# A sixth expert's weights outside the ring of block one

## The reference, cut to what matters

```python
def first_block(x, mem, ...):
    h = rms(x, mix_norm_g)                    # latent attention beside Hyena convolutions
    x = x + mixed @ w_out
    x = x + cross_attention(rms(x), rms(mem)) @ w_mo
    x = x + hier_moe(rms(x, ffn_norm_g), ...) # 32 experts, 2 per token
    return rms(x, final_norm_g)

def expert(t, e):                             # for the tokens routed to e
    a, b = t @ w_gate[e], t @ w_up[e]         # 1024 -> 256 twice
    return (silu(a) * b * combine[t, e]) @ w_down[e]   # 256 -> 1024

def second_block(x, c, ...):                  # RG-LRU beside block attention
    mod = silu(c) @ w_ada + b_ada             # 1024 -> 6 * 1024, scales and shifts
    x = layernorm(alpha * x + g1 * mixer(modulate(x, sh1, sc1)))
    return layernorm(alpha * x + g2 * moe(modulate(x, sh2, sc2)))
```

## Time and profile before

| what | value |
| --- | --- |
| median of 3 runs | 940.55 us (939.97 to 941.27) |
| profiled execution | 940.86 us, span 939.0 us |
| TensorE busy | 873.3 us, 93% of the span |
| VectorE, ScalarE, GpSimd busy | 505.8, 349.3, 22.3 us |
| HBM read | 286.70 MB, 306 GB/s over the span |
| SyncE's transfers | 25632 packets, 281.40 MB, 73.3% of the 16 engines' span |
| mean granted clock of TensorE | 0.994 |

### The profile page before, as it was taken

One profiled execution on the slowest core, in us unless ns is written; L12 is line 12 of the kernel. 1 busy time (PEld: TensorE's weight loads), 2 busy tenths in 40 slices (PEclk: granted clock), 3 DMA queues, 4 the chain that ended last, 5 costly groups with the idle time before them and its releaser, 6 DMA issues.

```text
span 939.0 us, 15033 instructions
## 1 busy us (share of the span) xinstructions
PE 873.3 (93%) x5670; PEld 562.7 (60%) x5670; DVE 505.8 (54%) x1110; ACT 349.3 (37%) x688; POOL 22.3 (2%) x41
## 2 busy tenths in 40 slices
PE   8999999999999998987887899999899999999995
PEld 7778558888867633443333379876665545545452
DVE  5876578466345657333322485788754633333335
ACT  5684444456345222221121366743621111111113
POOL 1010110000000000000000000000000000000000
PEclk9999999999999999999999999999999999999998
DMA  9655881545407999999999978530729999999991
GB/s 359 252 207 199 343 329 66 195 176 214 179 1 308 415 414 423 424 423 427 425 426 424 421 263 364 224 136 1 312 76 394 424 423 427 427 424 425 425 424 67
DMA packets 29184, 288.43 MB, mean 307 GB/s; under 512 B 3112, under 2 KB 5576, under 8 KB 7888
## 3 DMA queue, kind: packets, MB, share of 16 engines
q1 hardware_dynamic: 25632, 281.40, 73.3%
q0 software_dynamic: 1136, 3.74, 1.2%
q10 hardware_dynamic: 2368, 2.64, 0.8%
HBM read 286.70 MB, written 1.06 MB: 306 GB/s over the span
## 4 chain that ended last, share of the span: by engine, by line
PE 58%; DMA 19%; DVE 14%; ACT 4%; issue 3%; SPq 1%; DVEq 0%; ACTq 0%
DMA ring<-in_experts 15%; PE bank L1107 12%; PE bank L1127 7%; PE bank L703 7%; PE bank L705 6%; PE bank L704 6%; PE bank L1155 5%; DVE ring_r L525 3%; PE bank L1112 2%; DMA arena<-in_mem 2%; PE bank L1066 2%; PE bank L1119 2%; DMA ring<-in_ada 1%; DMA ring<-in_lat 1%; PE bank L794 1%
## 5 line engine op out<-in xcount | busy, mean ns | idle before, releaser
L525 DVE TENSOR_TENSOR ring_r<-ring,ring_r 128x1024 fp32r<-128x1024 f32 (+1 forms) x84 | 99.2, 1211 | 66.7 <-ACT ring_r L518 66.5
L1107 PE MATMUL bank<-ring,arena 128*64 128x256 f32 x1056 | 121.2, 382 | 1.6 <-DMA ring<-in_experts 1.4
L518 ACT ACTIVATE ring_r<-ring 128x1024 fp32r<-128x1024 f32 (+1 forms) x84 | 85.0, 1046 | 68.3 <-PE bank L705 67.6
L703 PE MATMUL bank<-HT_r,ring_r 128*128 128x256 f32 x352 | 101.8, 289 | 4.6 <-DVE ring_r L525 3.8
L705 PE MATMUL bank<-HT_r,ring_r 128*128 128x256 f32 x352 | 99.6, 283 | 0.0
L1107 PEld LDWEIGHTS bank<-ring,arena 128*64 128x64 f32 x1056 | 74.2, 137 | 39.3 <-issue 6.2
L1127 PE MATMUL bank<-ring,arena 128*64 128x512 f32 (+1 forms) x512 | 96.7, 604 | 0.5 <-DVE arena L2492 0.3
L1723 ACT ACTIVATE arena<-bank 128x256 f32<-128x256 f32 (+1 forms) x65 | 31.8, 490 | 147.5 <-PE bank L1107 83.4
L1112 PE MATMUL bank<-ring,arena 128*32 128x512 f32 x496 | 59.6, 598 | 25.1 <-DMA ring<-in_experts 25.1
L704 PE MATMUL bank<-XN_r,ring_r 128*128 128x256 f32 x288 | 81.5, 283 | 0.0
L2465 DVE SCALAR_TENSOR_TENSOR arena<-bank,arena,HT 128x512 f32<-128x512 f32 x33 | 24.8, 750 | 101.5 <-PE bank L1127 101.5
(11 more groups left out here) (483 smaller groups left out, 1425.8 us busy)
## 6 DMA issues: line engine op xcount, KB each, us to landing
ring<-in_experts SPq DMA_DIRECT2D x64, 2048.0 KB, 16.6
ring<-in_experts SPq DMA_DIRECT2D x64, 1024.0 KB, 14.0
ring<-in_ada SPq DMA_DIRECT2D x12, 2048.0 KB, 8.8
ring<-in_win SPq DMA_DIRECT2D x5, 2048.0 KB, 12.2
ring<-in_hy SPq DMA_DIRECT2D x3, 2048.0 KB, 18.3
ring<-in_mk SPq DMA_DIRECT2D x2, 2048.0 KB, 13.4
ring<-in_mv SPq DMA_DIRECT2D x2, 2048.0 KB, 9.3
ring<-in_wo SPq DMA_DIRECT2D x2, 2048.0 KB, 8.1
```

The costliest lines, as they stand in the source:

```text
L518: nc.scalar.activation(R(h), w, ACT.Copy).then_inc(sem("w_high"), 1)
L525: nc.vector.tensor_tensor(R(w), w, R(h), ALU.subtract).then_inc(sem("w_low"), 1)
L703: mm(ps, R(ah), R(bh), start=first, stop=False)
L1107: last = mm(gu_bank[g * wide:(g + 1) * wide, 0:256], xw[:, k, :], w[k // 4][:, o:o + 256], start=k == 0, stop=k == KD - 1)
```

## The change

Six experts are held instead of five, so block one's ring has 30 places (`RUNG`) for its experts instead of 31.

- Expert 4's down half goes into ROW, issued first of all experts' parts (after `skip_z` and the transposed mix, both long past). Its gate and up half stays in XN and HT.
- Expert 5 lies outside too: down half in X, issued when the first sorting bank is full, gate and up half in the arena (two parts, when the last one is).
- ada8 and ada9 are summed in one bank as one set; the sum of both is evacuated to a piece of the arena. ada8's slot is free once its matmuls are done, ada9's once the bank is full. The first four experts are loaded in the order 2, 0, 1, 3.
- X is overwritten in the sorting, so the four banks of the sums are begun in the routing (two on each side of the counts) and steps 1 and 2 have a filler instead. These banks are 1 to 4, so the eight sorting banks are now four, each used twice (5, 6, 7, 0). ScalarE copies banks 0, 1, 2, 3, 4 and 6 of them, VectorE 5 and 7.
- final_norm_g's row, which lies in ROW, is loaded by GpSimd after expert 4's down matmuls and no longer after the mix.
- Expert e from 6 on lies in slot (e-2) modulo 4 of the experts' places. The extra rounds' slot is the one of expert 30 (before: 29), and SyncE's wait ahead of them asks for a count of 31 (before: 30).

The diff, cut to its core:

```diff
-RUNG = [NE - 1, NE]
+RUNG = [NE - 2, NE]
...
-        + [(f"gx{b}", 8, ((3, 4, 5, 6, 7, 0, 1, 2), (4, 5, 6, 7, 4, 5, 6, 7))[b - 1])] \
+        + [(f"gx{b}", 8, ((5, 6, 7, 0, 5, 6, 7, 0), (4, 5, 6, 7, 4, 5, 6, 7))[b - 1])] \
...
-LAST.update({f"ada{_i}": (f"adac{_i}", 0) for _i in (6, 7, 8, 9, 11)})
-ADA_SETS = {_i: _s for _s in ((0, 7), (7, 8), (8, 9), (9, 10), (10, 12)) for _i in range(*_s)}
-ADA_DONE = {f"ada{_i}": _n + 1 for _n, _i in enumerate((0, 1, 2, 3, 4, 5, 10))}
+LAST.update({f"ada{_i}": (f"adac{_i}", 0) for _i in (6, 7, 11)})
+LAST["ada9"] = ("ada8", 0)
+ADA_SETS = {_i: _s for _s in ((0, 7), (7, 8), (8, 10), (10, 12)) for _i in range(*_s)}
+ADA_DONE = {f"ada{_i}": _n + 1 for _n, _i in enumerate((0, 1, 2, 3, 4, 5, 8, 10))}
...
-                for e in range(RING):
+                if b == 0:
+                    sp.wait_ge(sem("skip_z"), TT * ORDER)
+                    for j in range(2):
+                        k, use = place("mixT", j)
+                        sp.wait_ge(sem(f"bank_full{k}"), use + 1)
+                    sp.dma_start(outside[0][1], w[RING, :, GU:SLOT]).then_inc(sem("outside0"), 16)
+                for e in ((2, 0, 1, 3), range(RING))[b]:
...
+                    beside_ring(0)
+                    k, use = place("gx1", 0)
+                    sp.wait_ge(sem(f"bank_full{k}"), use + 1)
+                    sp.dma_start(outside[1][1], w[RING + 1, :, GU:SLOT]).then_inc(sem("outside1"), 16)
                     k, use = place("gx1", KD - 1)
                     sp.wait_ge(sem(f"bank_full{k}"), use + 1)
-                    sp.dma_start(fifth_down, w[RING, :, GU:SLOT]).then_inc(sem("fifth_down"), 16)
-                    for e in range(RING + 1, first):
-                        q = (e - 1) % RING
-                        last_user = e - RING - (e <= 2 * RING)
+                    beside_ring(1)
+                    for e in range(RING + 2, first):
+                        q = (e - 2) % RING
+                        last_user = e - RING - 2 * (e < 2 * RING + 2)
...
                 n = sp.value_load(tabi[0:1, XCOUNT:XCOUNT + 1], min_val=0, max_val=NX[b + 1] - 1)
-                sp.wait_ge(sem(f"down_done{b + 1}"), NE - RING + 2)
+                sp.wait_ge(sem(f"down_done{b + 1}"), NE - RING + 3 - b)
                 with sp.If(n > 0):
...
                 else:
-                    occupy("cnt1", 0, 8)
+                    start_sum((0, 1))
+                    occupy("cnt1", 0, 5)
...
-                if b == 2:
-                    start_sum((2, 3))
-                occupy(f"gx{b}", 0, 6 if b == 1 else 1)
+                start_sum((2, 3))
+                occupy(f"gx{b}", 0, 3 if b == 1 else 1)
...
-                        if b == 1 and isinstance(e, int) and e < 3:
-                            start_sum((2, 3) if e == 1 else (0, 1))
-                        elif b == 1:
+                        if b == 1:
...
-                for k in range(0, KD, 2):
+                for k in (0, 1, 2, 3, 4, 6) if b == 1 else range(0, KD, 2):
...
-            for j in range(2):
-                ready(pool, "mixT", j)
-            broadcast_row(ROW[:, 0:1024], "final_norm_g", D, "rows")
...
+            pool.wait_ge(sem("down_done1"), RING + 1)
+            broadcast_row(ROW[:, 0:1024], "final_norm_g", D, "rows")
```

More of the change, by code:

```diff
@@ L194 @@
     STAGES += [(f"xT{_h}", 1)] + ([(f"xs{_h + 2}", 1)] if _h + 2 < XH else []) + [(f"xv{_h}", 1)]
-STAGES += [("ada8", 1), ("mo", 4), ("ada9", 1)]
+STAGES += [("ada8", 1), ("mo", 4)]
 EXPERT = {1: (6, 7, 5, 0), 2: (4, 5, 6, 7)}
@@ L202, in _moe_stages @@
     one = b == 1
[L203 to L206 removed]
+    return [(f"rT{b}", 4, ((5, 6, 7, 0), (7, 4, 5, 6))[b - 1])] + [(f"rt{b}", 1, ((2,), (4,))[b - 1]), (f"rl{b}", 1, ((3,), (5,))[b - 1])] + [("adac9", 1, (0,))] * one \
+        + ([("cnt1", 1, (7,)), ("sct1", 4, (1, 2, 3, 4))] if one else [("sct2", 4, (0, 1, 2, 3)), ("cnt2", 1, (6,)), ("g2r", 2, (7, 4))]) \
+        + [(f"gx{b}", 8, ((5, 6, 7, 0, 5, 6, 7, 0), (4, 5, 6, 7, 4, 5, 6, 7))[b - 1])] \
+        + ([("bias", 1, (5,)), ("slots1", 1, (0,))] if one else [("slots2", 1, (5,))])
 STAGES += _moe_stages(1)
@@ L476, in vacated @@
                 if m <= prev < m + RUNG[b]:
-                    sp.wait_ge(sem(f"down_done{b + 1}"), prev - m + 1 + (RUNG[b] < NE and prev - m >= RING))
+                    sp.wait_ge(sem(f"down_done{b + 1}"), prev - m + 1 + (NE - RUNG[b]) * (prev - m >= RING))
                     return
@@ L527, in ada_sum @@
         def ada_sum(i):
-            return ring[:, slot(PLACE[f"ada{i}"]), 4096:4608]
+            return area(at + 3584, 512) if i == 9 else ring[:, slot(PLACE[f"ada{i}"]), 4096:4608]
         ssq_x, rstd_x = stat(2), stat(2)
@@ L593, in experts, with beside_ring @@
                     first = 3 * RING
+                    def beside_ring(n):
+                        for q in range(2):
+                            sp.dma_start(outside[n][0][q], w[RING + n, :, q * GU // 2:(q + 1) * GU // 2]
+                                         ).then_inc(sem(f"outside{n}"), 16)
                     sp.wait_ge(sem("xn_low"), TT)
@@ L1175, in down_arrived @@
                 def down_arrived(e, r):
-                    if b == 1 and isinstance(e, int) and e == RING:
-                        pe.wait_ge(sem("fifth_down"), 16)
-                        return fifth_down
+                    n = beside_ring(e)
+                    if n is not None:
+                        return outside[n][1]
                     q = rung(e, r)
-                    ahead = 16 * (NE // RING - (q == RING - 1)) if b == 2 else 0
-                    more = 0 if b == 1 and r == 0 and not (isinstance(e, int) and e < RING) else 16
+                    ahead = 16 * (NE // RING - (q >= RING - 2)) if b == 2 else 0
+                    more = 0 if b == 1 and r < 2 and not (isinstance(e, int) and e < RING) else 16
                     pe.wait_ge(sem(f"slot_down{q}"), (e - r) * (16 // RING) + more + ahead)
@@ L2384, in moe @@
                 if b == 1:
-                    modulation(8)
                     modulation(9)
@@ L2437, in moe @@
                 second = window(1, 1)
-                for k in range(1 if b == 1 else 3, KD, 2):
+                for k in range(5 if b == 1 else 3, KD, 2):
                     sorted_out(k)
```

26 lines of the change are left out of this document (11 added, 15 removed).

## The result

| | before | after |
|---|---|---|
| median of the runs on one chip | 941.37 us (939.08 to 945.41, 16 runs) | 944.17 us (941.64 to 947.42, 16 runs) |
| ratio to before | 1 | 1.0029, 95% interval 1.0015 to 1.0043 |
| span of the profiled execution | 939.0 us | 940.9 us |

The changed kernel is slower by 0.29%, 2.7 us. I had forecast no change (941.0) and held this side for the second likeliest.

What follows compares the result with a forecast made beforehand. DMA's weight stream was taken to bound block one's experts, then block two's modulation weights. 940.86 - 6.2 (S) + 6.5 (L) = 941.2, on the median's footing 940.9; forecast 941.0 us, range 937.3 to 944.5.

Steps and rivals of the forecast that it cites:

- T: Landing of the last expert's gate weights in block one, 528.2 us before the change; marks the end of the weight stream.
- S: How much earlier T comes because weights are carried before the stream is full: 6.2 us, bounds 5 to 8.
- The 2.7 us for an idle queue at 320.7: Taken off S: DMA has nothing left at 320.7, so the two arena parts land after 7.6 us, not 4.9.
- The two agree within their error, so the ring costs nothing more: Expert 10's down part: 6.3 us earlier by the ring, 6.0 by the stream, so no further deduction from S.
- after that expert the margin grows: After expert 10, TensorE's steps stay shorter than an expert's 7.4 us of loading until 408.3.
- L: How much longer from T to ada11's matmuls, as block two's loads wait for 31 counts: 6.5 us, bounds 4.9 to 9.
- The routing: Routing and sorting ahead of block one's experts: sums replacing fillers and four-bank sorting together change the time by 0.
- The clock: TensorE's clock probably falls to 1.2 GHz in the 7.2 us wait for ada10; cold work may fit before ada11.
- Rival 1: Block end: clock falls unhidden, or bias and gate tables take more DMA; L = 9, 943.4 us, slower; chance 0.27.
- Rival 2: Clock stays up in the routing (S = 7.7), ada11 comes without more sharing (L = 5.2); 938.1 us; chance 0.17.
- Rival 3: Block two's loads are not late, so S stays and L is 0; 934.4 us, faster; chance 0.06.
- my signs: Profile marks for being right, such as 4 MB carried from 256 to 283 and a 7 us wait for ada10.

Runs made afterwards that it cites:

- e1: The changed kernel with block two's first two weight loads (win0, ada10) issued ahead of SyncE's wait for 31 down counts: 934.95 us, ratio 0.9945 to before.
- e2: The kernel before with only SyncE's wait ahead of the extra-expert test raised from 30 to 31 down counts: 948.44 us, ratio 1.0084 to before.
- e3: The changed kernel with 22 filler matmuls instead of 4 ahead of ada10's matmuls: 942.57 us, ratio 1.0034 to before.
- e6: The changed kernel with only win0 issued ahead of SyncE's wait for 31 down counts: 936.34 us, ratio 0.9938 to before.
- e8: The changed kernel with ScalarE's two bias table loads moved behind its copies of ada11's sums: 943.54 us, ratio 1.0024 to before.
- e9: The changed kernel with both 22 fillers ahead of ada10's matmuls and the bias table loads behind ada11's sums: 942.65 us, ratio 1.0022 to before.
- e7: The changed kernel with block one's first four experts loaded in order 0, 1, 2, 3 instead of 2, 0, 1, 3: 946.09 us, ratio 1.0051 to before.
- e12: The changed kernel with win0 and ada10 issued first and VectorE's extra-expert lists moved into its idle time in steps 28 to 30: 933.62 us, ratio 0.9914 to before.
- e5: The kernel before with the change's routing sums, four-bank sorting, step fillers and PSUM banks, but old weights, ring and wait: 941.02 us, ratio 0.9991 to before.

## Why the prediction came out as it did

**The mechanism was right.** The gain at the start, the wait for 31 counts that takes it back, the idle engines, win0 at T + 5.0 (I had 5.1): all are in the profile, and e1 and e2 show each half by itself. What I forecast as "the same" was slower, because the two halves were closer in my sum than on the chip.

**S: 6.2 predicted, 4.7 measured** (258.0 - 253.3, the mean of the six profiles with the changed start and the old lists, after, e1, e3, e6, e8 and e9, which lie between 251.9 and 253.9). Against the profile of before as it stands it would be 6.0, so the miss is no larger than one shift. Inside the sum more went otherwise than I wrote. Counted by megabytes that have landed, the changed kernel's stream is ahead of the old one by 9.4 us at the 20th, 8.1 at the 24th, 6.9 at the 30th, 6.6 at the 33rd (expert 10's down part) and 5.1 at the 39th, and it stays there until the shift in before; 0.7 of all these is A's.
- The 2.7 us for an idle queue at 320.7 were not paid. The sorting began earlier, so the two arena parts were issued at 318.8 and 319.2, before X's part landed at 320.3. By my sum 7.2 would have been left at the 20th megabyte, and it was 9.4.
- 1.3 us went between the 20th and the 24th, with the engines at 422 GB/s from 336 to 344: a shift again, which I could not foresee, and whose cause is open. It took back over half of the 2.2 that the first point had given; that S came out near is in part luck.
- "The two agree within their error, so the ring costs nothing more", and "after that expert the margin grows": this step fails. Expert 10's down part did land at 361.00 + 6.2 = 367.2, as predicted (367.5). But the ring holds back the part behind it too: expert 11's is issued at 368.0, and the engines carry 378 GB/s from 370 to 380. Those 0.46 MB are 1.1 us, and the lead falls by 1.5 over the next two experts. I had set a bound of the bytes beside one of the ring and, when they agreed, read it as neither costing; here two limits of one size made a queue that ran below full between them. How much of the 1.5 us is the ring's stays open: from expert 10's landing to T it is 154.4 us after the change and 152.9 in e7 and e12, where the stream is full, but also 154.4 in before, where it is full and a shift lies between, and 152.8 in e3 and e9, where the ring is as after the change.

**L is right in size partly by luck.** Predicted 6.5; measured 25.4 - 19.1 = 6.3, or 7.8 against the profile's own 17.6. I had put ada11 at T + 24.1 and it came at T + 25.4 (24.8 to 25.6 in the other profiles with the late wait): 1.3 too short. And I had taken T before with the shift in it, which made the end before 17.6 and not 19.1: 1.5 too short. S was worked out from bytes and landings and doesn't use T, so nothing cancels there; the two mistakes cancel each other inside L. With 19.1 my forecast would have been 1.5 us lower, 939.5, and further off. The step that made T + 24.1 too short is the restart: win0 took 8.8 us into an idle queue and not the 7.6 of the earlier trace rows (8.2 to 9.2 in e2, e3, e8 and e9). ada10 followed after 5.8 and ada11 after 5.8, for 5.1 and 6.3 in my sum. The extra time that I gave the bias table is there, but not by the table (e9).

**The routing: 0 predicted, 1.3 us gained** in the profile (sorting 1.9 earlier, 0.6 of that ahead of the change). The clock stayed at 1.00 from 304 to 306, where it had been 0.50 (its first microsecond is in the earlier trace rows); in e5, with the same order of TensorE's work, it is 1.00 too. e5 has T - A lower by 1.1 for the whole of this half.

**The clock** fell at the new wait, as predicted (0.50), and cost nothing, as predicted for the case that the cold work fits in front of ada11. The Trainium skill ("TensorE: Matmul & The Clock Gate", HAM oscillation) describes the cold burst behind a wait for DMA; the trace agrees (3.38 us for 1.92 after 8.93 us of waiting). e3 shows that 18 fillers more prevent it here and gain nothing.

**Rival 1** named 943.4 and came nearest in time, but neither of its causes holds (e3, e8, e9). The even turns of queues, which it took from the Trainium skill ("DMA: Bandwidth & Descriptors", Queues, rings and completion order) as an estimate of 3 us, did not show either: taking away 1.5 MB of rival traffic moved ada11 by 0 to 0.6 us. **Rival 2** had the routing's gain right, but not its S of 7.7 or its L of 5.2. **Rival 3** had said that the full gain needs the loads to pass SyncE's test; e1 makes them do so and is at 0.9945, 5.2 us (3.4 to 7.0) for the 6.2 it promised.

Of my signs, one failed: between 256 and 283 the engines carry 3.2 MB and not 4, because ROW's part came before 256.8. The others held, with the wait for ada10 at 8.9 us and not 7, and ada11's matmuls at 547.0 and not 546.

What stays open: the ratio gives the change +2.7 us, and the two starts of ada11's matmuls, counted from A, give +1.9; a difference of 0.8 is less than one shift. Open too are what causes the shifts, and how much of S the ring took.

## What to carry to other kernels

When a change takes one place out of a ring, look at every wait that counts places: the loads behind the last such wait are issued one step later, and if the stream runs dry in that step it costs the gap and the restart. Put loads that have a place already ahead of a test that has to wait. When two bounds come out equal, don't read that as neither costing: look for stretches below full and for what else feeds the nearer bound (here list making on VectorE, for which TensorE waited 3.1 us; moved into idle time it cost nothing). Look at where landings shift before reading 1 us from two profiles. And take TensorE's PSUM banks as part of the critical path when work is moved across them.

## What the runs showed of the hardware

- A 2 MB load issued into an idle queue landed after 8.2 to 9.2 us when more of 2 MB stood behind it (win0 in after, e2, e3, e7, e8, e9), and after 7.2 to 7.6 when it stood with one of 1 MB (before, after); in a full stream an expert of 3 MB takes 7.4.
- After TensorE's wait of 2.0 us in step 7 the granted clock over 360 to 370 was 0.83 (after, e9) and 0.86 (e7), but 1.00 in e1 and e3 with the same wait. One such wait can leave the clock up or not, in kernels that are alike there.
- The time at which ada8's matmuls start, with no edit ahead of it, scattered from 268.0 to 270.0 us between profiles. An effect of 1 us is read from one profile only against a mark near by.
- In a full stream all landings of SyncE's queue can shift by 1.3 to 1.5 us at once and stay shifted, with the engines at 415 to 428 GB/s: at 513.4 in before, at 343.5 in after, at 381.6 in e1.
